# First attention with one cos/sin table: rope queries from doubled weight columns, scores over 128 rows

## The chip, the cores and the metric

The kernel runs on one NeuronCore of a Trainium2 chip. The metric is the device time of one execution in microseconds, lower is better. TensorE is called PE here (its weight loads PEld), VectorE DVE, ScalarE ACT, GpSimd POOL and the queue that issues the transfers SP.

## The reference

Three layers on 512 tokens of width 2048, all in float32: a latent attention with 16 heads, a sliding-window attention, and a mixer of stick-breaking attention and a linear recurrence. The change touches the first. Cut to what matters:

```python
proj = h @ w_in                       # c_q 512, c_kv 512, k_rope 64, gate 2048 columns
q = (rmsnorm(c_q, q_norm) @ w_uq).reshape(B, S, 16, 128 + 64)
q_nope, q_rope = q[..., :128], rope(q[..., 128:], positions, 64)
kv = (rmsnorm(c_kv, kv_norm) @ w_ukv).reshape(B, S, 16, 128 + 128)
k_nope, v = kv[..., :128], kv[..., 128:]
k_rope = rope(k_rope, positions, 64)  # one for all heads
s = (q_nope . k_nope + q_rope . k_rope) * 192 ** -0.5      # causal, softmax, times v
# rope, halves x1, x2 of 32 dims: [x1 * cos - x2 * sin, x2 * cos + x1 * sin]
```

The result is multiplied by silu(gate) and goes through an output projection.

## The kernel before, in words

Every float32 matmul of a projection is done as three: each operand is split into a rounded upper part (hi, ACT) and the rest (lo, DVE), and hi x hi, hi x lo and lo x hi are added up in PSUM. Weights come in tiles of 1 MB into two raw buffers, are split in four pieces of 128x512 each (`hi` L465 on ACT, `lo` L475 on DVE), and `multiply` (L482) runs a piece: four chunks of 128 rows, three matmuls of 512 tokens each (L490 to L492). Which columns of the raw buffer a piece reads is said by `raw_piece` (L451).

Each engine runs its own program; the order is written out by hand. `STEPS` (L82) lists the steps of each engine in each phase, and one counting semaphore per engine (T, A, V, G) tells the others how far it is. The phases: `load`, `in` (nine tiles of the input projection, the ninth holding the 64 rope key columns in its upper half), `mla` (16 heads and one more body), and then the output projection and the other two layers. The `mla` body i does the attention of head i-1 and the projections of head i, interleaved:

- PE (`mla_T`, L910): scores of head i-1 for the query blocks 3, 2, 1, 0, each with three matmuls for the 128 nope rows and three for the 64 rope rows (partitions 64 to 127); gate piece 0; transposes of v; gate piece 1; transposes of the probabilities of block 3 (`turn`, L942); gate piece 2; blocks 2 and 1; gate piece 3; QR, the rope queries (the piece holds 64 nope columns too, so that it has 128); block 0; QN; two matmuls with the rotation matrix into `pt[1]` (L968, L969); KN; probabilities times v (PV); V.
- DVE (`mla_V`, L1041): mask, row maximum and its negative for each block, two weight pieces, normalisation of the probabilities, lower halves, the gate, then `qr` copied out of PSUM, its lower half (`qt_lo`), the lower half of the nope queries, `rope_V` (L880: product with the sine, product with the cosine, sum), the lower half of the rotated queries, and keys.
- ACT (`mla_A`, L986): exponentials, the upper halves, tanh for the gate.

In the phase `in` the same rotation is done once for the keys (`in_T` L773, `in_A` L810, `in_V` L834), between the gate pieces of head 0; behind it DVE does two reciprocals (`rq`, `rkv`), two fills and the first pieces of head 0. Cosine and sine come from two angle computations of nine DVE steps each (`angle_V`, L730) and two ACT sines.

Of the kernel before, what the change touches and what calls it, by code (L numbers as in the profile page):

```python
# [14 lines left out]
P = 128  # L15
# [46 lines left out]
NCONST = columns(CONST, [("ident", P), ("ones", P), ("freq", 2), ("eps", 1), ("one", 1), ("rot1", P), ("causal", P),  # L62
# [29 lines left out]
        "T": "norm norms turn rq_tok".split(),  # L92
        "A": ("root hi0 sq0 hi1 sq1 hi2 sq2 cos hi3 sq3 hi4 sq4 sin hi5 sq5 hi6 sq6 hi7 sq7 rot kt_hi root_q "
              "root_kv kr_hi").split(),
        "V": ("rstd ev0 lo0 ev1 lo1 a00 a01 a02 a03 a04 a05 a06 a07 r0 ev2 lo2 ev3 lo3 a10 a11 a12 a13 a14 a15 "
              "a16 a17 r1 ev4 lo4 ev5 lo5 ev6 lo6 ev7 lo7 ev8 kt_lo k_sin k_cos kr kr_lo rq rkv scale z1 z2").split(),
# [8 lines left out]
    "kv": {
        "T": "norm rows dup0 dup1 dup2 dup3 rstd_tok v0 v1".split(),
        "A": "root dup k_hi0 cos sin k_hi1 kd_hi0 kd_hi1 kd_hi2 kd_hi3 v_hi0 v_hi1".split(),
        "V": ("rstd ev0 k_lo0 pos sinks a00 a01 a02 a03 a04 a05 a06 a07 r0 a10 a11 a12 a13 a14 a15 a16 a17 r1 "
              "ev1 k_lo1 ev2 k_sin0 k_cos0 kr0 kd_lo0 k_sin1 k_cos1 kr1 kd_lo1 k_sin2 k_cos2 kr2 kd_lo2 k_sin3 "
              "k_cos3 kr3 kd_lo3 ev3 scale v_lo0 v_lo1 z1 z2").split(),  # L110
        "G": "z1 z2".split(),
    },
    "swa": {
        "T": "s00 s01 s10 s11 t00 t01 pv0 t10 t11 turn pv1".split(),
        "A": ("exp00 exp01 exp02 exp03 sink0 tanh exp10 exp11 exp12 exp13 sink1 pt_hi00 pt_hi01 qt_hi pt_hi10 "
              "pt_hi11 q_hi").split(),
        "V": ("gate mask00 top00 scaled00 minus00 mask01 top01 scaled01 minus01 mask10 top10 scaled10 minus10 "
              "sum0 inv0 norm0 mask11 top11 scaled11 minus11 silu pt_lo00 pt_lo01 sum1 inv1 norm1 q_ev qt_lo "
              "pt_lo10 pt_lo11 q_sin q_cos qr q_lo y").split(),
        "G": "keys sink pair".split(),  # L120
    },
# [9 lines left out]
    "stick": {
        "T": "z t3 t2 t1 t0 lru pv q_norm k_norm vt".split(),
        "A": ("tanh_s abs0 abs1 abs2 abs3 exp ln weights xc_hi w_hi pt_hi3 pt_hi2 pt_hi1 pt_hi0 tanh_l tanh_r "
              "tanh_i q_sq a tanh_a m q_root q_hi k_sq k_root k_hi v_hi").split(),
# [3 lines left out]
              "kn k_lo v_lo").split(),  # L138
# [111 lines left out]
def constants():  # L250
# [14 lines left out]
    c[:, CONST["rot1"]] = rotation(ROPE1, ROPE1)  # L265
# [20 lines left out]
def build(nc, x, positions, sinks, params, consts, w, out):  # L286
# [6 lines left out]
    with ExitStack() as ctx:  # L293
# [29 lines left out]
        with ExitStack() as scope:  # L323
            c_hi, c_lo = sb("c_hi", [P, 2 * RC, S], F32R, scope), sb("c_lo", [P, 2 * RC, S], F32R, scope)
            cos, sin = sb("cos", [P, S], F32, scope), sb("sin", [P, S], F32, scope)
# [15 lines left out]
            angle, turns, acc_q, acc_kv = kn, prob[:, 0:S], acc, prob[:, S:2 * S]  # L341
# [109 lines left out]
        def raw_piece(tile, p):  # L451
            r = raw[:, tile.slot, :]
            if tile.phase == "mla" and tile.k == 1:
                nq, nk = NOPE + ROPE1, NOPE + V1
                uq = r[:, 0:RC * nq].rearrange("p (c n) -> p c n", c=RC)
                ukv = r[:, RC * nq:RC * (nq + nk)].rearrange("p (c n) -> p c n", c=RC)
                return [uq[:, :, nq - P:nq], uq[:, :, 0:P], ukv[:, :, 0:P], ukv[:, :, P:2 * P]][p]
            if tile.phase == "out3":
                p = (p + PIECES // 2) % PIECES
            return r[:, p * PIECE:(p + 1) * PIECE].rearrange("p (c n) -> p c n", n=P)  # L460

        def split(buf, slot):
            return buf[:, slot, :].rearrange("p (c n) -> p c n", n=P)
# [261 lines left out]
        def angles_V(q, psum, freq, cos_arg, sin_arg, tmp):  # L725

            for n, arg in enumerate((cos_arg, sin_arg)):
                angle_V(q, n, psum, freq, arg, tmp)

        def angle_V(q, n, psum, freq, arg, tmp):  # L730
            shift = (0.25, 0.0)[n]
# [7 lines left out]
            q.eng.tensor_scalar(tmp, arg, shift, magic, ALU.add, ALU.add).then_inc(*q.did(f"a{n}1"))  # L739
# [11 lines left out]
            q.eng.tensor_scalar(arg, arg, float(np.pi / 2) * 4 * shift, 3.14159250, ALU.add, ALU.min).then_inc(*q.did(f"a{n}7"))  # L751
# [21 lines left out]
        def in_T(q):  # L773
# [22 lines left out]
            q.eng.matmul(pt[1][:, :], rot_hi[:, :], qr_hi[:, :], start=True, stop=False)  # L796
            q.eng.matmul(pt[1][:, :], rot_hi[:, :], qr_lo[:, :], start=False, stop=True).then_inc(*q.did("turn"))
# [12 lines left out]
        def in_A(q):  # L810
            q.body("in", 0)
            for k in range(KROPE + 1):
# [11 lines left out]
                if k in (2, 4):  # L824
                    q.eng.wait_ge(*q.at(f"V.r{k // 2 - 1}"))
                    q.eng.activation(((cos, sin)[k // 2 - 1])[:, :], (angle[:, :], turns)[k // 2 - 1], ACT.Sin).then_inc(*q.did(("cos", "sin")[k // 2 - 1]))
            q.eng.activation(rot_hi[:, :], c("rot1"), ACT.Copy).then_inc(*q.did("rot"))
# [3 lines left out]
            q.eng.wait_ge(*q.at("V.kr"))  # L831
            copy_hi(q, kr_hi[:, :], turned, "kr_hi")

        def in_V(q):  # L834
            q.body("in", 0)
            for k in range(KROPE + 1):
# [14 lines left out]
                dst = c_raw[:, k % 2, :] if k < KROPE else qr[:, :]  # L851
                q.eng.tensor_tensor(dst, pp[k % 2][:, :], rstd[:, :], ALU.mult).then_inc(*q.did(f"ev{k}"))
# [11 lines left out]
            q.eng.wait_ge(*q.at(f"G.sum{KROPE - 1}"))  # L864
# [14 lines left out]

        def rope_V(q, plain, turned_psum, source, name):  # L880

            q.eng.wait_ge(*q.at(source))
            q.eng.tensor_tensor(turned, turned_psum[:, :], sin[:, :], ALU.mult).then_inc(*q.did(f"{name}_sin"))
            q.eng.tensor_tensor(plain[:, :], plain[:, :], cos[:, :], ALU.mult).then_inc(*q.did(f"{name}_cos"))
            q.eng.wait_ge(*q.at(f"V.{name}_cos"))
            q.eng.tensor_tensor(turned, turned, plain[:, :], ALU.add).then_inc(*q.did(f"{name}r"))
# [23 lines left out]
        def mla_T(q, i, proj, attn):  # L910
# [10 lines left out]
            if attn:  # L921
                q.eng.wait_ge(*q.at("V.kn_lo", i - 1))
                q.eng.wait_ge(*q.at("V.qr_lo", i - 1))
                for b in reversed(range(NB)):
# [3 lines left out]
                    r = slice(P // 2, P)  # L928
# [1315 lines left out]
```

## Time and profile before

| | us |
|---|---|
| median of 3 runs | 2397.55 |
| lowest and highest | 2395.2, 2397.93 |
| profiled execution | 2396.43 |
| its span | 2394.6 |
| PE busy | 2314.2 (97%) |
| DVE busy | 1494.8 (62%) |
| ACT busy | 957.8 (40%) |

Times in the rows are microseconds from the start of the span. PE's matmuls are pipelined: the duration of one is longer than the distance to the next, so the cost of a matmul in a stream is read from the distances between starts. A form like 64*128 names the rows and columns of the weights.

### The profile page before, as it was taken

What the parts mean: (1) busy time and instruction counts of PE and PEld (TensorE: products, weight loads), DVE (VectorE), ACT (ScalarE), POOL (GpSimd) and SP (SyncE); (2) the same over time, 40 slices, a digit from 0 to 9 for tenths busy, and PEclk for the clock granted to TensorE, in tenths of its full rate; (3) what the DMA queues carried; (4) which work ended last, traced back from release to release, by engine and by line L of the source; (5) the groups of instructions that cost most, each with busy time, mean ns of one, the idle gap of its engine ahead of it and who ended that gap; (6) DMA issues with size and microseconds to landing.
All of it is one profiled execution on the core that took longest, in us unless ns stands there. A gap on an engine that the chain in (4) does not pass through costs nothing.

```text
span 2394.6 us, 32256 instructions
## 1 busy us (share of the span) xinstructions
PE 2314.2 (97%) x10724; PEld 1880.1 (79%) x10724; DVE 1494.8 (62%) x2580; ACT 957.8 (40%) x1870; POOL 193.2 (8%) x226
## 2 busy tenths in 40 slices
PE   7999999999999999999999989989999999997999
PEld 5877788777778878888888878867888888885887
DVE  6556666666643377777777753377666766766332
ACT  5333334333422244444444442255344444444222
POOL 4100000000021101000000031140000000002000
PEclk8999999999999999999999989999999999998999
DMA  6322222222353343222222263432323324233633
GB/s 218 104 66 75 71 60 70 74 74 74 110 176 88 123 118 93 79 79 79 79 79 79 63 218 92 140 93 77 111 72 103 99 84 114 71 98 110 186 95 105
DMA packets 379438, 239.21 MB, mean 100 GB/s; under 512 B 4868, under 2 KB 353284, under 8 KB 379398
## 3 DMA queue, kind: packets, MB, share of 16 engines
q1 hardware_dynamic: 379398, 238.71, 34.6%
q8 instruction: 21, 0.34, 0.1%
q14 instruction: 19, 0.16, 0.0%
HBM read 210.12 MB, written 28.57 MB: 100 GB/s over the span
## 4 chain that ended last, share of the span: by engine, by line
PE 91%; DVE 6%; ACT 1%; POOL 1%; issue 1%; DMA 0%; SPq 0%; DVEq 0%; ACTq 0%
PE pp L490 26%; PE pp L492 25%; PE pp L491 25%; PE ps L511 3%; PE ps L512 2%; PE ps L513 2%; POOL act_lo L1157 1%; DVE act_lo L1756 1%; PE pt L948 1%; DVE w_lo L479 1%; PE po L511 1%; PE po L513 1%; PE po L512 1%; DVE act_lo L709 1%; PE po L1486 1%
## 5 line engine op out<-in xcount | busy, mean ns | idle before, releaser
L490 PE MATMUL pp<-act_hi,w_hi 128*128 128x512 f32 x2496 | 1006.2, 403 | 30.8 <-POOL act_lo L1157 10.2
L492 PE MATMUL pp<-act_hi,w_lo 128*128 128x512 f32 x2496 | 980.2, 393 | 0.0
L491 PE MATMUL pp<-act_lo,w_hi 128*128 128x512 f32 x2496 | 977.7, 392 | 0.0
L479 DVE TENSOR_TENSOR w_lo<-raw,w_hi 128x512 fp32r<-128x512 f32 x692 | 475.0, 725 | 250.2 <-ACT w_hi L473 249.3
L490 PEld LDWEIGHTS pp<-act_hi,w_hi 128*128 128x128 f32 x2496 | 471.8, 189 | 146.0 <-issue 25.1
L492 PEld LDWEIGHTS pp<-act_hi,w_lo 128*128 128x128 f32 x2496 | 471.3, 189 | 102.8
L491 PEld LDWEIGHTS pp<-act_lo,w_hi 128*128 128x128 f32 x2496 | 472.9, 189 | 96.9 <-issue 5.0
L473 ACT ACTIVATE w_hi<-raw 128x512 fp32r<-128x512 f32 x692 | 397.1, 620 | 87.0 <-DMA raw<-w_out 53.7
L1157 POOL TENSOR_TENSOR act_lo<-y_whole,act_hi 128x512 fp32r<-128x512 f32 x36 | 49.1, 1397 | 1132.3 <-ACT act_hi L1151 1132.3
L1541 ACT ACTIVATE s_prob<-ps,s_minus,s_q_scale 128x256 f32<-128x256 f32 x128 | 70.9, 558 | 140.8 <-DVE s_minus L1614 140.8
L1261 DVE TENSOR_TENSOR xT<-pp,xT 128x512 f32 (+1 forms) x32 | 22.1, 691 | 167.6 <-PE pp L492 167.6
L1220 ACT ACTIVATE square<-xT 128x512 f32 (+1 forms) x32 | 20.2, 633 | 255.3 <-DVE xT L1261 255.3
L490 PE MATMUL pp<-c_hi,w_hi 128*128 128x512 f32 x256 | 103.3, 404 | 1.2 <-DVE w_lo L479 0.7
L492 PE MATMUL pp<-c_hi,w_lo 128*128 128x512 f32 x256 | 101.7, 397 | 0.0
L491 PE MATMUL pp<-c_lo,w_hi 128*128 128x512 f32 x256 | 101.7, 397 | 0.0
L1001 ACT ACTIVATE prob<-ps,minus,q_scale 128x512 f32<-128x512 f32 (+1 forms) x64 | 39.0, 615 | 126.4 <-DVE minus L1063 126.4
L1284 POOL TENSOR_TENSOR acc<-acc,square 128x512 f32<-128x512 f32 x30 | 38.8, 1293 | 288.6 <-ACT square L1220 288.6
L490 PEld LDWEIGHTS pp<-c_hi,w_hi 128*128 128x128 f32 x256 | 48.6, 190 | 13.6 <-DVE pT_lo L878 1.1
L492 PEld LDWEIGHTS pp<-c_hi,w_lo 128*128 128x128 f32 x256 | 48.4, 189 | 11.8
L491 PEld LDWEIGHTS pp<-c_lo,w_hi 128*128 128x128 f32 x256 | 48.5, 190 | 10.1
L504 ACT ACTIVATE pT_hi<-pt 128x512 fp32r<-128x512 f32 (+1 forms) x64 | 26.2, 436 | 58.3 <-PE pt L948 58.3
L1605 DVE TENSOR_TENSOR ps<-ps,s_con 128x512 f32<-128x512 f32 x64 | 44.4, 694 | 3.4 <-PE ps L513 3.4
(362 smaller groups left out, 2709.3 us busy)
## 6 DMA issues: line engine op xcount, KB each, us to landing
raw<-w_in SPq DMA_DIRECT2D x48, 1024.0 KB, 5.8
raw<-swa_w_in SPq DMA_DIRECT2D x36, 1024.0 KB, 5.6
raw<-mla_w_in SPq DMA_DIRECT2D x25, 1024.0 KB, 5.8
raw<-mla_w_out SPq DMA_DIRECT2D x16, 1024.0 KB, 6.0
raw<-swa_w_out SPq DMA_DIRECT2D x16, 1024.0 KB, 5.9
raw<-w_out SPq DMA_DIRECT2D x16, 1024.0 KB, 7.4
x_feature_major<-xT SPq DMA_DIRECT2D x12, 1024.0 KB, 7.8
xT<-x_feature_major SPq DMA_DIRECT2D x3, 3584.0 KB, 16.4
```

The lines of the kernel that those rows point to most:

```text
L473: q.eng.activation(split(w_hi, tile.piece_slot(p)), raw_piece(tile, p), ACT.Copy).then_inc(s_hi, 1)
L479: q.eng.tensor_tensor(split(w_lo, s), raw_piece(tile, p), split(w_hi, s).bitcast(F32), ALU.subtract).then_inc(s_lo, 1)
L490: q.eng.matmul(psum[:, :], wh, ah, start=start and n == 0, stop=False)
L491: q.eng.matmul(psum[:, :], wh, al, start=False, stop=False)
L492: last = q.eng.matmul(psum[:, :], wl, ah, start=False, stop=stop and n == PIECE // P - 1)
L511: q.eng.matmul(psum, a[0], b[0], start=start, stop=False)
L512: q.eng.matmul(psum, a[0], b[1], start=False, stop=False)
L513: return q.eng.matmul(psum, a[1], b[0], start=False, stop=stop)
L1001: q.eng.activation(prob[:, OFF[b]:OFF[b] + w_], SCORE[b][:, 0:w_], ACT.Exp, bias=minus[:, b:b + 1], scale=q_scale[:, b:b + 1], accum_out=t ...
L1157: q.eng.tensor_tensor(act_lo[:, j, :], y_whole[:, j, :], act_hi[:, j, :].bitcast(F32), ALU.subtract).then_inc(s_ylo_g if j < Y_GPSIMD else ...
L1541: q.eng.activation(s_prob[:, h, b * 2 * P:(b + 1) * 2 * P], BANKS[h][half][:, b % 2 * 2 * P:(b % 2 + 1) * 2 * P], ACT.Exp, bias=s_minus[:, ...
L1605: q.eng.tensor_tensor(bank, bank, band, ALU.add).then_inc(*q.did(f"mask{h}{half}"))
```

## The change: what it does

The rotation matrix and the cosine and sine tables of the first layer go. The rope query piece is made of the 64 rope columns taken twice, so that its product holds x1, x2, x1, x2 in four groups of 32 rows. One table, `rope_table`, holds cos, cos, sin, -sin in these rows: one angle computation with a shift per row (constants `turns` and `phase`) and one sine. The queries are that product times the table, over 128 rows. For the keys the same is done once, with the table times the norm, and the constant `fold` (128x128 of zeros and ones) adds the four groups up so that every group of 32 rows holds the right half of the rotated key; two matmuls with it take the place of the keys' two rotation matmuls. The scores' rope part then runs over all 128 rows. In the heads the two rotation matmuls, three products and sums and one pair of hi and lo go. Weight pieces are read and written through a pattern with one dimension more (`whole`, `twice`). Step tables of other phases are only moved or wrapped anew.

```diff
-            cos, sin = sb("cos", [P, S], F32, scope), sb("sin", [P, S], F32, scope)
+            rope_table = sb("rope_table", [P, S], F32, scope)
-                return [uq[:, :, nq - P:nq], uq[:, :, 0:P], ukv[:, :, 0:P], ukv[:, :, P:2 * P]][p]
+                return [twice(uq[:, :, NOPE:nq]), whole(uq[:, :, 0:P]), whole(ukv[:, :, 0:P]), whole(ukv[:, :, P:2 * P])][p]
...
+        def twice(half):
+            return half.unsqueeze(2).to_broadcast([P, PIECE // P, 2, ROPE1])
+        def whole(chunks):
+            return chunks.rearrange("p c (d n) -> p c d n", d=2)
         def split(buf, slot):
-            return buf[:, slot, :].rearrange("p (c n) -> p c n", n=P)
+            return buf[:, slot, :].rearrange("p (c d n) -> p c d n", n=ROPE1, d=2)
@@ in_T
-            q.eng.matmul(pt[1][:, :], rot_hi[:, :], qr_hi[:, :], start=True, stop=False)
-            q.eng.matmul(pt[1][:, :], rot_hi[:, :], qr_lo[:, :], start=False, stop=True).then_inc(*q.did("turn"))
+            q.eng.matmul(pt[1][:, :], fold_hi[:, :], qr_hi[:, :], start=True, stop=False)
+            q.eng.matmul(pt[1][:, :], fold_hi[:, :], qr_lo[:, :], start=False, stop=True).then_inc(*q.did("fold"))
@@ in_A
-            q.eng.wait_ge(*q.at("V.kr"))
-            copy_hi(q, kr_hi[:, :], turned, "kr_hi")
+            q.eng.wait_ge(*q.at("T.fold"))
+            copy_hi(q, kr_hi[:, :], pt[1][:, :], "kr_hi")
@@ in_V
-                if k in (1, 3):
-                    angle_V(q, k // 2, pt[0][:, :], c("freq", 0), (angle[:, :], turns)[k // 2], root[:, :])
+                    angle_V(q, 0, pt[0][:, :], c("freq", 0), angle[:, :], root[:, :], c("turns", 0), c("phase", 0))
+                if k == 3:
+                    q.eng.wait_ge(*q.at("A.table"))
+                    q.eng.tensor_tensor(scaled_table, rope_table[:, :], rstd[:, :], ALU.mult).then_inc(*q.did("scaled"))
-            rope_V(q, qr, pt[1], "T.turn", "k")
-            sub_lo(q, kr_lo[:, :], turned, kr_hi[:, :], "kr_lo")
+            sub_lo(q, kr_lo[:, :], pt[1][:, :], kr_hi[:, :], "kr_lo")
@@ mla_T
-                    r = slice(P // 2, P)
-                    m = products(q, SCORE[b][:, 0:n], (qr_hi[r, t_], qr_lo[r, t_]), (kr_hi[r, 0:n], kr_lo[r, 0:n]), False, True)
+                    m = products(q, SCORE[b][:, 0:n], (qr_hi[:, t_], qr_lo[:, t_]), (kr_hi[:, 0:n], kr_lo[:, 0:n]), False, True)
-                q.eng.wait_ge(*q.at("V.qt_lo"))
-                q.eng.matmul(pt[1][:, :], rot_hi[:, :], qr_hi[:, :], start=True, stop=False)
-                q.eng.matmul(pt[1][:, :], rot_hi[:, :], qr_lo[:, :], start=False, stop=True).then_inc(*q.did("turn", rest=not attn))
+                q.eng.wait_ge(*q.at("V.qr"))
                 up_piece(KN, pp[1])
+                if not attn:
+                    q.eng.wait_ge(*q.at("T.rq_tok", phase="in", body=0))
+                    q.eng.sem_inc(*q.did("pv"))
@@ mla_A
-                q.eng.wait_ge(*q.at("V.qr_ev"))
-                copy_hi(q, qr_hi[:, :], qr[:, :], "qt_hi")
+                q.eng.wait_ge(*q.at("V.qr"))
+                copy_hi(q, qr_hi[:, :], qr[:, :], "qr_hi")
-                q.eng.wait_ge(*q.at("V.qr"))
-                copy_hi(q, qr_hi[:, :], turned, "qr_hi")
@@ mla_V
-                q.eng.tensor_copy(qr[:, :], pp[1][:, :]).then_inc(*q.did("qr_ev"))
+                q.eng.tensor_tensor(qr[:, :], pp[1][:, :], rope_table[:, :], ALU.mult).then_inc(*q.did("qr"))
-                rope_V(q, qr, pt[1], "T.turn", "q")
-                q.eng.wait_ge(*q.at("A.qr_hi"))
-                sub_lo(q, qr_lo[:, :], turned, qr_hi[:, :], "qr_lo")
```

## Rows read from the trace of the kernel before

**Rows 1.** Chain that ended last, whole span, shares by line.

```profile
by line: PE pp L490 25.8%; PE pp L492 25.3%; PE pp L491 25.2%; PE ps L511 2.9%; PE ps L512 1.7%; PE ps L513 1.7%; POOL act_lo L1157 1.0%; DVE act_lo L1756 0.9%; issue 0.7%; PE pt L948 0.7%; DVE w_lo L479 0.7%; PE po L511 0.6%; PE po L513 0.
```

**Rows 2.** Windows: bounds, length, busy of each engine, PE clock, DMA share, GB/s.

```profile
145.00:168.30 23.30, 18.42 (x72) 13.75 (x71) 17.83 (x24) 7.00 (x12) 0.00 (x0) 0.93 0.30 85
231.47:263.05 31.58, 31.58 (x150) 25.13 (x149) 20.83 (x43) 12.03 (x26) 0.00 (x0) 1.00 0.25 71
```

**Rows 3.** Timeline of PE in one head's scores: start, duration, line, form.

```profile
231.24 0.40 PE L492 MATMUL pp<-c_hi,w_lo 128*128 128x512 f32 x1
231.47 0.39 PE L511 MATMUL ps<-kn_hi,qn_hi 128*128 128x512 f32 x1
...
231.93 0.39 PE L513 MATMUL ps<-kn_hi,qn_lo 128*128 128x512 f32 x1
232.25 0.50 PE L511 MATMUL ps<-kr_hi,qr_hi 64*128 64x512 f32 x1
232.58 0.39 PE L512 MATMUL ps<-kr_lo,qr_hi 64*128 64x512 f32 x1
232.82 0.39 PE L513 MATMUL ps<-kr_hi,qr_lo 64*128 64x512 f32 x1
...
233.42 0.34 PE L512 MATMUL ps<-kn_lo,qn_hi 128*128 128x384 f32 x1
233.59 0.34 PE L513 MATMUL ps<-kn_hi,qn_lo 128*128 128x384 f32 x1
...
236.45 0.28 PE L512 MATMUL ps<-kr_lo,qr_hi 64*128 64x256 f32 x1
236.56 0.27 PE L513 MATMUL ps<-kr_hi,qr_lo 64*128 64x256 f32 x1
...
237.10 0.40 PE L491 MATMUL pp<-act_lo,w_hi 128*128 128x512 f32 x1
```

**Rows 4.** Timelines of DVE and PEld in that head, and the maxima by tile.

```profile
236.87 0.30 DVE L1057 TENSOR_TENSOR ps<-ps,con 128x128 f32<-128x128 f32 x1 [1.30 <-PE ps L513]
...
242.10 0.49 DVE L1075 TENSOR_SCALAR prob<-prob,inv 128x512 f32<-128x512 f32 x1
242.64 0.44 PEld L948 LDWEIGHTS pt<-con,prob 128*128 128x128 f32 x3
L1059 DVE TENSOR_REDUCE top<-ps x60: 290/490/692, 170.4 to 616.5; 128x1 f32<-128x512 f32 x15, 128x1 f32<-128x384 f32 x15, 128x1 f32<-128x256 f32 x15, 128x1 f32<-128x128 f32 x15
```

**Rows 5.** Waits of PE in the run-in, then timelines of DVE and ACT there.

```profile
PE pt L968 <- DVE qr_lo L507: 2.3, 1, 2.3
PE pt L802 <- DVE y_out L869: 1.4, 1, 1.4
140.86 0.69 DVE L883 TENSOR_TENSOR square<-pt,sin 128x512 f32<-128x512 f32 x1 [2.75 <-PE pt L797]
...
158.36 0.68 DVE L1097 COPY qr<-pp 128x512 f32<-128x512 f32 x1
142.91 0.63 ACT L504 ACTIVATE kr_hi<-square 128x512 fp32r<-128x512 f32 x1 [2.94 <-DVE square L886]
```

**Rows 6.** Timeline of PE: projection KN, first and last head's scores; DVE's kn_lo.

```profile
161.19 0.39 PE L490 MATMUL pp<-c_hi,w_hi 128*128 128x512 f32 x1
...
168.32 0.39 PE L511 MATMUL ps<-kn_hi,qn_hi 128*128 128x512 f32 x1
...
641.70 0.39 PE L511 MATMUL ps<-kn_hi,qn_hi 128*128 128x512 f32 x1
261.18 0.69 DVE L507 TENSOR_TENSOR kn_lo<-qr,kn_hi 128x512 fp32r<-128x512 f32 x1 [0.70 <-ACT kn_hi L504]
```

**Rows 7.** Timeline of GpSimd behind the last head.

```profile
654.23 16.74 POOL L1157 TENSOR_TENSOR act_lo<-y_whole,act_hi 128x512 fp32r<-128x512 f32 x12 [525.88 <-ACT act_hi L1151]
```

**Rows 8.** Lower weight parts by tile: in the heads, then in the output projection.

```profile
L479 DVE TENSOR_TENSOR w_lo<-raw,w_hi x120: 677/684/694, 177.5 to 633.0; 128x512 fp32r<-128x512 f32 x120
L479 DVE TENSOR_TENSOR w_lo<-raw,w_hi x63: 676/678/1467, 671.4 to 831.6; 128x512 fp32r<-128x512 f32 x63
```

More of the change, by code:

```diff
@@ L59, in columns @@
     return at
-NCONST = columns(CONST, [("ident", P), ("ones", P), ("freq", 2), ("eps", 1), ("one", 1), ("rot1", P), ("causal", P),
+NCONST = columns(CONST, [("ident", P), ("ones", P), ("freq", 2), ("eps", 1), ("one", 1), ("fold", P), ("turns", 1), ("phase", 1), ("causal", P),
                          ("rot2", P), ("dup", 2 * P), ("rotdup", 2 * P), ("band", 3 * 2 * P), ("strict", P),
@@ L91 @@
     "in": {
[L92 to L96, printed above, removed]
+        "T": "norm norms fold rq_tok".split(),
+        "A": ("root hi0 sq0 hi1 sq1 hi2 sq2 table hi3 sq3 hi4 sq4 hi5 sq5 hi6 sq6 hi7 sq7 kt_hi root_q root_kv "
+              "kr_hi").split(),
+        "V": ("rstd ev0 lo0 ev1 lo1 a00 a01 a02 a03 a04 a05 a06 a07 r0 ev2 lo2 ev3 lo3 scaled ev4 lo4 ev5 lo5 ev6 "
+              "lo6 ev7 lo7 ev8 kt_lo kr_lo rq rkv scale z1 z2").split(),
         "G": "sum0 sum1 sum2 sum3 sum4 sum5 sum6 sum7".split(),
@@ L99 @@
     "mla": {
-        "T": "s3 s2 s1 s0 vt t3 t2 t1 t0 turn pv".split(),
-        "A": "exp3 exp2 exp1 exp0 v_hi pt_hi3 pt_hi2 pt_hi1 tanh pt_hi0 qt_hi qn_hi qr_hi kn_hi".split(),
+        "T": "s3 s2 s1 s0 vt t3 t2 t1 t0 pv".split(),
+        "A": "exp3 exp2 exp1 exp0 v_hi pt_hi3 pt_hi2 pt_hi1 tanh pt_hi0 qr_hi qn_hi kn_hi".split(),
         "V": ("mask3 top3 minus3 mask2 top2 mask1 top1 mask0 top0 minus inv3 norm3 inv0 norm2 norm1 norm0 v_lo "
-              "pt_lo3 pt_lo2 pt_lo1 gate qr_ev pt_lo0 qt_lo qn_lo q_sin q_cos qr qr_lo kn_ev kn_lo y silu v").split(),
-    },
@@ L105 @@
[L105 to L121, printed above, removed]
@@ L131 @@
[L131 to L134, printed above, removed]
[3 rows of a table removed]
-              "kn k_lo v_lo").split(),
+              "pt_lo3 pt_lo2 pt_lo1 gate qr pt_lo0 qr_lo qn_lo kn_ev kn_lo y silu v").split(),
     },
@@ L148 @@
     },
+    "kv": {
+        "T": "norm rows dup0 dup1 dup2 dup3 rstd_tok v0 v1".split(),
+        "A": "root dup k_hi0 cos sin k_hi1 kd_hi0 kd_hi1 kd_hi2 kd_hi3 v_hi0 v_hi1".split(),
+        "V": ("rstd ev0 k_lo0 pos sinks a00 a01 a02 a03 a04 a05 a06 a07 r0 a10 a11 a12 a13 a14 a15 a16 a17 r1 ev1 "
+              "k_lo1 ev2 k_sin0 k_cos0 kr0 kd_lo0 k_sin1 k_cos1 kr1 kd_lo1 k_sin2 k_cos2 kr2 kd_lo2 k_sin3 k_cos3 "
+              "kr3 kd_lo3 ev3 scale v_lo0 v_lo1 z1 z2").split(),
+        "G": "z1 z2".split(),
+    },
+    "swa": {
+        "T": "s00 s01 s10 s11 t00 t01 pv0 t10 t11 turn pv1".split(),
+        "A": ("exp00 exp01 exp02 exp03 sink0 tanh exp10 exp11 exp12 exp13 sink1 pt_hi00 pt_hi01 qt_hi pt_hi10 "
+              "pt_hi11 q_hi").split(),
+        "V": ("gate mask00 top00 scaled00 minus00 mask01 top01 scaled01 minus01 mask10 top10 scaled10 minus10 sum0 "
+              "inv0 norm0 mask11 top11 scaled11 minus11 silu pt_lo00 pt_lo01 sum1 inv1 norm1 q_ev qt_lo pt_lo10 "
+              "pt_lo11 q_sin q_cos qr q_lo y").split(),
+        "G": "keys sink pair".split(),
+    },
     "out2": {
@@ L264, in rotation @@
         return r
-    c[:, CONST["rot1"]] = rotation(ROPE1, ROPE1)
+    half = ROPE1 // 2
+    fold = np.array([[1, 0, 0, 1], [0, 1, 1, 0], [0, 1, 1, 0], [1, 0, 0, 1]], np.float32)
+    c[:, CONST["fold"]] = np.kron(fold, np.eye(half, dtype=np.float32))
+    c[:, CONST["turns"].start] = np.array([0.25, 0.25, 0.0, 0.5])[p // half]
+    c[:, CONST["phase"].start] = 2 * np.pi * np.array([0.25, 0.25, 0.0, 0.5])[p // half]
     rot2 = c[:, CONST["rot2"]] = rotation(HD2, ROPE2)
@@ L339, in build @@
             gate, th = square[:, 0, :], root
-            angle, turns, acc_q, acc_kv = kn, prob[:, 0:S], acc, prob[:, S:2 * S]
+            angle, scaled_table, acc_q, acc_kv = kn, prob[:, 0:S], acc, prob[:, S:2 * S]
             c_raw, rstd_q, root_q = y_out, y_out[:, 0, :], y_out[:, 1, :]
@@ L738, in angle_V @@
             q.eng.wait_ge(*q.at(f"V.a{n}0"))
-            q.eng.tensor_scalar(tmp, arg, shift, magic, ALU.add, ALU.add).then_inc(*q.did(f"a{n}1"))
+            q.eng.tensor_scalar(tmp, arg, turns, magic, ALU.add, ALU.add).then_inc(*q.did(f"a{n}1"))
             q.eng.wait_ge(*q.at(f"V.a{n}1"))
@@ L823, in in_A @@
                     q.eng.activation(square[:, k % 2, :], c_raw[:, k % 2, :], ACT.Square).then_inc(*q.did(f"sq{k}"))
[L824 to L827, printed above, removed]
+                if k == 2:
+                    q.eng.wait_ge(*q.at("V.r0"))
+                    q.eng.activation(rope_table[:, :], angle[:, :], ACT.Sin).then_inc(*q.did("table"))
+            q.eng.activation(fold_hi[:, :], c("fold"), ACT.Copy)
             copy_hi(q, qr_hi[:, :], qr[:, :], "kt_hi")
@@ L878, in in_V @@
             q.eng.memset(pT_lo[:, hidden].bitcast(F32), 0.0).then_inc(*q.did("z2"))
[L880 to L886, printed above, removed]
         def in_G(q):
```

58 lines of the change are left out of this document (33 added, 25 removed), and 3 rows, old and new, of the table STEPS.

## The prediction

> **What bounds the kernel now.** I read the chain of waits first, then the windows by stage, then the timeline of one head. The chain that ended last lies for 76.3% on the three matmul lines of the weight helper, on TensorE (PE) [rows 1]. Within the first attention one head's window of 31.58 us shows PE busy for all of it, VectorE (DVE) for 20.83 and ScalarE (ACT) for 12.03 [rows 2], so what a head costs is what PE issues, not what the others do. The time from the first head's scores, 168.32, to the last head's, 641.70 [rows 6], is 15 periods of 31.56 us.
>
> Busy is not the same as streaming, though. In the timeline of PE the start-to-start distance tells the price of a matmul. Between two 128x512 matmuls over all 128 rows it is 0.23 us (231.24 to 231.47, and twice that to 231.93), at 384 columns 0.17 (233.42 to 233.59) and at 256 columns 0.11 to 0.12 (236.45 to 236.56) [rows 3]. Where the rope part of the scores begins (form 64*128, half the rows) the distance is 0.32, then 0.33 to its second matmul, together 0.19 more than twice 0.23. Going back, the two distances from 232.82 to 233.42 hold 0.60, of which 0.23 and 0.17 are the matmuls' own, 0.20 more [rows 3]. So each change between 128 and 64 rows opens a hole of about 0.195 us, in two halves. There are eight changes in a head, since four query blocks each go there and back, the last back into the gate's projection.
>
> The run-in is bound otherwise. From 145 to the first scores PE is busy 18.42 of 23.30 us, at a mean clock of 0.93 [rows 2]: there it waits on the split and normalisation chains of DVE and ACT, and the longest of its waits is 2.3 us, for the lower half of the rope queries ahead of the rotation [rows 5].
>
> **Part 1: scores over 128 rows.** The number and the columns of the matmuls stay: 24 per head. Without holes the section would take 6 x (0.231 + 0.173 + 0.118 + 0.118) = 3.84 us. Measured from 231.47 to 237.10, the second matmul of the gate behind it, it is 5.63; less the one 0.231 distance of the gate that lies in it, 5.40 [rows 3]. Difference 1.56 us a head: 8 x 0.195. A matmul over twice the rows is taken at the same time, since the 128-row ones of the same block and columns stream at 0.23, 0.17 and 0.12 and the third rope matmul (232.58 to 232.82, 0.24) isn't faster for having half the rows [rows 3]. Bounds of this part: 0 (the holes stay, for a reason other than the rows) and 1.56; I take 1.56, because the step from the projection's buffers to the scores', 231.24 to 231.47, also changes every operand and has no hole.
>
> Here the Trainium skill has a rule. TensorEngine Tiling (Array Packing), Key Properties, says that a change of tiling mode, not merely of tile, drains TensorE; it gives no price, and the holes of [rows 3] are what it would look like. By it the sum is the same.
>
> **Part 2: what is late next.** Softmax starts from the end of the scores: DVE's mask of block 1 runs at 236.87 after an idle 1.30 us that PE ends, and the normalisation of block 3's probabilities runs from 242.10 for 0.49, to 242.59. PE's weight load for the transposes of that block starts at 242.64, right behind it [rows 4]. So PE already reaches these transposes just as they become ready. Everything from the mask to the normalisation moves with the scores' end, and so does PE's way there (gate piece 0, four transposes of v, gate piece 1), except that the last of the eight holes lies on PE's way and not on the mask's: it is gone for PE alone. PE therefore arrives 0.19 us earlier than the probabilities and waits that long. Is the mask still released by the scores, now that they end 1.4 us sooner behind block 3's? The last matmul of the section would start at 231.47 + 3.84 - 0.12 = 235.19, and the mask 0.31 behind it (236.56 to 236.87 now), at 235.50. DVE's work on blocks 3 and 2 stands ahead: two masks of 0.30, two maxima of at most 0.69 [rows 4] and a one-column step, which I estimate at 0.2, 2.2 us. It starts behind block 3's last matmul, which begins at 231.47 + 5 x 0.231 = 232.63, by 0.31 and 0.11 for twice the columns (256/2.4 GHz): 233.05, and ends at 235.25. It just holds, by 0.25 us. I take 0.2 lost a head, bounds 0 and 0.5 (0.3 more if DVE isn't done). Net of parts 1 and 2: 1.36 a head.
>
> **Part 3: the rotation goes.** Two matmuls of 128x512 a head at 0.23 each [rows 3]: 0.46 us of PE. Nothing waits there in a steady head. The new wait in its place, KN's projection on DVE's product of the queries with the table, stands behind QN's twelve matmuls, 2.8 us after QR's end, where the product takes one DVE step as the copy does now (0.68, [rows 5]); it is met with about 2 us to spare. DVE loses four 0.69 us steps a head (two products, a sum, one subtraction) and ACT one copy of 0.63. All are hidden under PE and count nothing, apart from this: kn_lo, for which the next scores wait, now ends at 261.87 [rows 6], 1.2 us ahead of them (231.47 + 31.56 = 263.03), and will have over 2 us.
>
> Steady head: 31.56 - 1.36 - 0.46 = 29.74. Over 15 periods 27.3 us. The range of a period is 29.4 (no new wait, 0.2 better, and a little) to 30.2.
>
> **Part 4: the first head and what stands before it.** Two steps. In the keys' chain DVE's three products after the fold vanish: ACT's kr_hi starts at 142.91 now and could start when the first product does, 140.86 [rows 5]. That is 2.05 us off a chain that runs on DVE through two reciprocals and six weight splits to QR, QN and the gate, the 1.4 us wait of the transposes [rows 5] being a part of the same delay. So QR, QN and the queries' step end 2.05 sooner: 158.36 + 0.68 - 2.05 = 156.99. KN waits for that, not for the subtraction and rotation behind it; it begins at 161.19 now [rows 6], so 4.15 us earlier, with 1.0 us of the old 2.3 us wait left. Then the clock. From KN's first matmul to the first scores 24 matmuls take 168.32 - 161.19 = 7.13 us [rows 6], 5.55 at 0.231, and the granted clock of this stretch is 0.93 [rows 2]: part of the 24, right after the 2.3 us wait, ran at 1.2 instead of 2.4 GHz. With the longest wait at 1.0 us I take full speed, 1.58 saved, for a total of 5.7. Bounds: 2.5 (the chain is held by the weight splits' ACT side, and the clock falls as before) and 6.5 (the 1.0 wait gone too).
>
> The second angle computation (nine DVE steps) and second sine go, and one product for the scaled table comes: they lie under the nine input tiles, where PE doesn't wait. Value 0, bounds 0 and 0.5.
>
> **Part 5: the last head's tail.** Its scores also shorten, by 1.5 us. Behind them PE isn't the bound: the chain goes softmax, transposes, ACT, and from 654.23 through GpSimd's 12 subtractions, 16.74 us [rows 7]. It starts from the scores' end, so it moves with it, unless the stored y arrives too late (it is asked for independently of the scores). I take 1.4; bounds 0 and 1.6.
>
> **Part 6: weight splits everywhere.** All 692 pairs of hi and lo now go through a pattern with one more dimension, and the rope piece reads each half chunk twice. In the heads, where half of the pieces read a strided source, a lo takes 684 ns; in the first output stage, all contiguous, 678 [rows 8]. The pattern costs 6 ns at most, so I take 0; bounds 0 and 0.05 us a piece, which PE hides in the heads. The chain of waits has the lo's line for 0.7% of the span [rows 1], 16.8 us or 24.5 pieces, so that even the upper bound costs 1.2 us there, and 1.6 more in part 2's softmax (2 pieces in each of 16 heads).
>
> **Sum** in the profiled execution: 27.3 + 5.7 + 1.4 = 34.4 us off a span of 2394.6, that is 2360.2, and 1.8 around it as now (2396.43 - 2394.6) gives 2362.0. The median of the three runs is 1.1 above the profiled one: 2363.1.
>
> **Rivals.**
> A. *The holes stay.* They could belong to a switch of operands rather than of rows. Then 15 x 0.46 + 5.7 = 12.6: 2385. Against it: a change of all operands at full rows is seamless (part 1). Chance 0.07.
> B. *The softmax takes it back.* If DVE's work on blocks 3 and 2, or ACT's exponentials, sets the mask and not the scores' end, PE waits at the transposes for most of the 1.56. With 1.0 a head lost instead of 0.2: 15 x 0.8 = 12 less gained, 2375. For it: the margin of 0.25 us in part 2 and a load that starts 0.05 behind the normalisation. Chance 0.12.
> C. *Slower: the splits.* If the extra dimension or the doubled read costs x us a piece, the loss is (24.5 + 32) x. It outweighs 34.4 from x = 0.61, so nearly a doubling of 0.68; at exactly double, 38 us, 2401. The strided row against the contiguous one speaks against it [rows 8]. Chance 0.03.
> D. *Slower: weight loads of full height show.* If the load of a 128-row weight could not lie under the matmul before it, 12 loads of 0.19 in 16 heads would add 36 us: 2399. The kn matmuls load the same height in the same section at 0.23 apart (231.47 to 231.93). Chance 0.01. The Trainium skill, TensorE: Matmul & The Clock Gate, The mechanism (Part 3), does say that weight loads overlap running matmuls only where their row group differs; this trace disagrees, with 0.23 us between matmuls of one row group, each with a load of its own.
> E. *The doubling isn't what it says*, the rotation gone and something of equal size in its place, or a wait that I don't see: within 0.2% of now. Chance 0.02.
> My forecast has the remaining 0.75, its own range 2358 to 2370.
>
> **Range and chances.** A measurement of this kernel tells about 0.2% (4.8 us) from no change. The range for 8 in 10: down to 2356 (no new wait, 3 us; run-in and tail at their best, 1; and 3 for a run's level), up to 2376, which takes B in and leaves A, C, D and E out with what the forecast's own range misses. Faster: forecast, A and B, 0.94, and half a point of the rest; same 0.02; slower 0.04.
>
> **What would show it.** In the profile after: the rope matmuls' form is 128*128 and all of a block's six start at equal distances; the scores' section is 3.8 to 3.9 us from first to next projection; a head takes 29.7; PE waits 0.2 at the transposes of block 3, released by DVE's normalisation. The first scores start near 162.6, with a granted clock near 1.00 before them. Splits still take 0.62 and 0.68. Wrong would be: a hole that stays at the change from qn to qr weights (A); a wait of near 1 us at the transposes (B); a first head at half clock, which takes 1.6 back.

## The result, and the profile after

| | before, us | changed, us |
|---|---|---|
| median (4 runs each) | 2397.74 | 2359.8 |
| lowest and highest | 2395.2, 2398.92 | 2358.55, 2361.89 |
| profiled execution | 2396.43 | 2360.93 |
| its span | 2394.6 | 2359.1 |

The ratio of changed to before is 0.9844, 95% interval 0.9827 to 0.9861: 1.6% faster, 35.5 us in the two profiled executions. The forecast was 2363, with 2356 to 2376.

The windows of the run-in and of one head, as in [rows 2] (bounds, length, busy of PE, PEld, DVE, ACT, POOL, PE clock, DMA share, GB/s):

```profile
145.00:162.63 17.63, 16.23 (x71) 12.29 (x69) 13.11 (x20) 4.71 (x7) 0.00 (x0) 1.00 0.30 88
221.87:251.49 29.62, 29.62 (x148) 24.72 (x146) 18.27 (x38) 11.41 (x25) 0.00 (x0) 1.00 0.26 75
```

A head now takes 29.62 us, all of it PE's; DVE has gone from 20.83 to 18.27 and ACT from 12.03 to 11.41, which bought nothing by itself (the runs below show it). The run-in to the first scores is 17.63 instead of 23.30 us long, at the full granted clock. The timeline of PE in the scores of that head, to be laid beside [rows 3], with the start of the transposes of v behind the gate piece:

```profile
221.64 0.40 PE L503 MATMUL pp<-c_hi,w_lo 128*128 128x512 f32 x1
221.87 0.39 PE L522 MATMUL ps<-kn_hi,qn_hi 128*128 128x512 f32 x1
...
222.33 0.39 PE L524 MATMUL ps<-kn_hi,qn_lo 128*128 128x512 f32 x1
222.55 0.39 PE L522 MATMUL ps<-kr_hi,qr_hi 128*128 128x512 f32 x1
222.78 0.39 PE L523 MATMUL ps<-kr_lo,qr_hi 128*128 128x512 f32 x1
223.01 0.39 PE L524 MATMUL ps<-kr_hi,qr_lo 128*128 128x512 f32 x1
...
223.40 0.34 PE L523 MATMUL ps<-kn_lo,qn_hi 128*128 128x384 f32 x1
223.58 0.34 PE L524 MATMUL ps<-kn_hi,qn_lo 128*128 128x384 f32 x1
...
225.60 0.28 PE L524 MATMUL ps<-kr_hi,qr_lo 128*128 128x256 f32 x1
...
225.95 0.40 PE L502 MATMUL pp<-act_lo,w_hi 128*128 128x512 f32 x1
...
228.46 0.60 PE L939 MATMUL pt<-con,acc 128*128 128x128 f32 x4
```

The rope products (kr, qr) have the form 128*128. From the last nope product to the first rope one it is 0.22 us (222.33 to 222.55), where it was 0.32, and back (223.01 to 223.40, two distances) 0.39 instead of 0.60. From 221.87 to 225.95 the section takes 4.08, which is 3.85 without the gate's first matmul, against 5.40.

DVE, PE and PEld in that head, as in [rows 4]:

```profile
225.92 0.30 DVE L1057 TENSOR_TENSOR ps<-ps,con 128x128 f32<-128x128 f32 x1 [0.44 <-PE ps L524]
...
231.15 0.49 DVE L1075 TENSOR_SCALAR prob<-prob,inv 128x512 f32<-128x512 f32 x1
...
231.41 0.39 PE L503 MATMUL pp<-act_hi,w_lo 128*128 128x512 f32 x1
231.69 0.42 PEld L949 LDWEIGHTS pt<-con,prob 128*128 128x128 f32 x4 [0.31 <-DVE prob L1075]
232.11 0.48 PE L501 MATMUL pp<-act_hi,w_hi 128*128 128x512 f32 x1
```

The mask still follows PE (idle 0.44 us, released by the scores). The normalisation of block 3 ends at 231.64 and the weight load for its transposes, which in an unbroken stream would start with the matmul of 231.41, starts at 231.69 after an idle 0.31 us. That is the new wait.

The run-in, as in [rows 5] and [rows 6]: PE's waits, ACT's kr_hi, KN's first matmul, the first and the last head's scores, and GpSimd behind the last head, as in [rows 7]:

```profile
PE pp L501 <- DVE qr L1097: 0.8, 1, 0.8
140.77 0.60 ACT L515 ACTIVATE kr_hi<-pt 128x512 fp32r<-128x512 f32 x1 [0.82 <-PE pt L807]
156.92 0.50 PE L501 MATMUL pp<-c_hi,w_hi 128*128 128x512 f32 x1 [0.79 <-DVE qr L1097]
...
162.63 0.39 PE L522 MATMUL ps<-kn_hi,qn_hi 128*128 128x512 f32 x1
...
606.89 0.39 PE L522 MATMUL ps<-kn_hi,qn_hi 128*128 128x512 f32 x1
618.09 16.74 POOL L1155 TENSOR_TENSOR act_lo<-y_whole,act_hi 128x512 fp32r<-128x512 f32 x12 [489.75 <-ACT act_hi L1149]
```

The span's 35.5 us by these marks: the first scores come 168.32 - 162.63 = 5.69 us sooner; 15 periods take 606.89 - 162.63 = 444.26 instead of 473.38, 29.12 less (29.617 a head against 31.559); from the last head's scores to GpSimd's first subtraction it is 11.20 instead of 12.53, 1.33 less. That makes 36.1. Everything behind, which the change doesn't touch, took 0.6 longer in this execution.

### The profile page after: what moved, and what is told of

Same layout as the page of the kernel before. It is cut to its first block, busy times and chain, and to the rows that moved or that the text cites. A ratio compares the mean times of both kernels' runs of the same rounds, so it can differ in the third digit from the quotient of the medians.

```text
span 2359.1 us, 32060 instructions
## 1 busy us (share of the span) xinstructions
PE 2277.1 (97%) x10692; PEld 1868.9 (79%) x10692; DVE 1441.4 (61%) x2505; ACT 947.6 (40%) x1853; POOL 193.8 (8%) x226
## 4 chain that ended last, share of the span: by engine, by line
PE 90%; DVE 6%; ACT 1%; POOL 1%; issue 1%; DMA 0%; SPq 0%; DVEq 0%; ACTq 0%
PE pp L501 26%; PE pp L503 26%; PE pp L502 26%; PE ps L522 2%; PE ps L523 2%; PE ps L524 2%; POOL act_lo L1155 1%; DVE act_lo L1754 1%; PE pt L949 1%; DVE w_lo L490 1%; PE po L522 1%; PE po L523 1%; PE po L524 1%; DVE act_lo L720 1%; PE po L1486 1%
## 5 line engine op out<-in xcount | busy, mean ns | idle before, releaser
L518 DVE TENSOR_TENSOR s_pT_lo<-pt,s_pT_hi 128x512 fp32r<-128x512 f32 x64 | 36.9, 618 | 18.2 <-ACT s_pT_hi L515 18.2
```

## The experiments

Each gives the time of one execution unless a median is named. The run-in's start drifts from run to run by up to 1.4 us (the first of the matmuls that sum the latent norms starts at 135.62 us in the changed kernel's first profile, at 137.05 in its second), so times in the first head are told from there.

**Half of the rows again.**

```diff
+ r = slice(64, 128)
- (qr_hi[:, t_], qr_lo[:, t_]), (kr_hi[:, 0:n], kr_lo[:, 0:n])
+ (qr_hi[r, t_], qr_lo[r, t_]), (kr_hi[r, 0:n], kr_lo[r, 0:n])
```

> The changed kernel, but the rope products of the scores take rows 64 to 127 alone (half of the rope sum is left out). Everything else, the missing rotation included, stays. My theory (each change of the number of rows opens a hole of 0.195 us on PE): eight holes a head are back, the section of the scores takes 5.4 us instead of 3.85, a head 31.1 instead of 29.62, and the profiled execution 2361 + 15 x 1.45 + 1.3 = 2384 us. Rival (the holes came with the old rope operands, queries that passed a rotation and a sum): no holes, 29.6 a head, 2361 us.

Measured: 2386.4 us, a head 31.10. The timeline of PE at the first change of rows:

```profile
225.76 0.40 PE L524 MATMUL ps<-kn_hi,qn_lo 128*128 128x512 f32 x1
226.09 0.50 PE L522 MATMUL ps<-kr_hi,qr_hi 64*128 64x512 f32 x1
226.42 0.39 PE L523 MATMUL ps<-kr_lo,qr_hi 64*128 64x512 f32 x1
```

0.33 and 0.33 again: the holes are back, without any rotation in the kernel. The section of the scores takes 5.40 us as before (225.31 to 230.94, less 0.23), and a head 1.49 more than in the changed kernel. The rival falls.

**The lower half.** The same edit with `slice(0, 64)`.

> As the run on the upper half, but with rows 0 to 63 (the other half of the rope sum is left out). My theory (the number of rows counts, not where they lie): the same as with the upper half, 31.1 us a head and 2384. Rival (a product that starts at row 64 is what stalls): rows 0 to 63 begin where the full products begin, so no holes, 29.6 a head and 2361.

Measured: 2386.3 us, a head 31.09.

```profile
225.60 0.39 PE L524 MATMUL ps<-kn_hi,qn_lo 128*128 128x512 f32 x1
225.92 0.49 PE L522 MATMUL ps<-kr_hi,qr_hi 64*128 64x512 f32 x1
226.25 0.39 PE L523 MATMUL ps<-kr_lo,qr_hi 64*128 64x512 f32 x1
```

The same 0.32 and 0.33. What counts is that the number of rows changes, not where the half lies.

**Part 1 alone, in the kernel before.**

```diff
- r = slice(P // 2, P)
+ r = slice(0, P)
```

> The kernel before, with its rotation, but the rope products of the scores run over all 128 rows (rows 0 to 63 add products that don't belong to the scores). This is part 1 of the change alone. My theory: no holes, the section 3.85 us, 0.1 of it given back as a wait at the transposes of block 3, a head 31.56 - 1.44 = 30.1 us, the first head as before (first scores at 168.3), the profiled execution 2396.4 - 15 x 1.44 - 1.3 = 2373.5. Rival (the holes need the rotation gone too): 2396.

Measured: 2374.0 us, a head 30.07, first scores where they were. 1.49 us a head come from the rows alone, and of the time 22.6 us (2396.56 for the run of before beside it, less 2374.0) of the 35.5.

**Four changes of rows instead of eight.** The kernel before, products sorted:

```diff
- for b in (3, 2, 1, 0): nope(b), rope(b)
+ nope(3), nope(2), rope(3), rope(2), rope(1), nope(1), nope(0), rope(0)
```

> The kernel before, rope products on 64 rows as before, but in another order: nope 3, nope 2, rope 3, rope 2, rope 1, nope 1, nope 0, rope 0. That is four changes of rows instead of eight with the same 24 products. My theory: price per change 0.195, so 0.78 off a head, section 4.62 instead of 5.40, a head 30.8, 2396.4 - 15 x 0.78 = 2384.7, and 0.8 less in the last head, 2384; up to 0.3 a head may come back, because block 3 is ready later (2388). Rival (each rope group costs its two halves, wherever it stands): no gain, 2396.

Measured: 2383.8 us, a head 30.77: 0.79 less than before, 0.198 for each change left out. The timeline of PE where two rope groups follow each other, and where the rows change back:

```profile
232.09 0.39 PE L513 MATMUL ps<-kr_hi,qr_lo 64*128 64x512 f32 x1
232.32 0.34 PE L511 MATMUL ps<-kr_hi,qr_hi 64*128 64x384 f32 x1
...
233.09 0.28 PE L513 MATMUL ps<-kr_hi,qr_lo 64*128 64x256 f32 x1
233.30 0.39 PE L511 MATMUL ps<-kn_hi,qn_hi 128*128 128x256 f32 x1
233.52 0.28 PE L512 MATMUL ps<-kn_lo,qn_hi 128*128 128x256 f32 x1
```

Rope 3 to rope 2 is 0.23 us, no hole; rope 1 to nope 1 is 0.21 and 0.22 where 256 columns take 0.12. The price belongs to the change and not to the rope group. This is also the smaller cure: an order of issue alone gives a good third of the change (12.8 of 35.5 us, one execution beside one of before at 2396.56).

**The first head's wait as it was.**

```diff
  up_piece(QN, pp[0])
- q.eng.wait_ge(*q.at("V.qr"))
+ q.eng.wait_ge(*q.at("V.qr_lo"))
  up_piece(KN, pp[1])
```

> The changed kernel, but PE waits ahead of KN for the lower half of the rope queries (as the old rotation did) instead of for the product alone. In a steady head this wait is met (29.62 a head stays). In the first head it ends 1.5 us later (156.9 to 158.4 us), so PE's wait there is 2.3 instead of 0.8. My theory of the first head (4.1 us of the 5.7 from the shorter chain, 1.6 from the clock, which fell after a wait of 2.3): the clock falls again, and the first scores start at 162.6 + 1.5 + 1.6 = 165.7, granted clock about 0.94 there; 2364 us. Rival (the clock has to do with something else in the old run-in, for instance the longer wait of the transposes ahead): full clock, 164.1, 2362.4.

Measured: 2363.4 us, a head 29.62. PE's wait and the window from KN to the first scores, then the first two matmuls in it:

```profile
PE pp L501 <- DVE qr_lo L518: 2.3, 1, 2.3
158.84:166.00 7.16, 7.16 (x25) 5.75 (x25) 3.04 (x5) 0.78 (x2) 0.00 (x0) 0.77 0.57 149
158.84 0.80 PE L501 MATMUL pp<-c_hi,w_hi 128*128 128x512 f32 x1 [2.31 <-DVE qr_lo L518]
...
160.28 0.63 PE L501 MATMUL pp<-c_hi,w_hi 128*128 128x512 f32 x1
```

The granted clock over these 24 matmuls is 0.77 (0.76 in the kernel before, 1.00 in the changed one), and the first seven of them take 0.63 us or more: from 159.43 on they start 0.43 apart instead of 0.23, the half rate, 1.2 GHz. KN starts 1.52 us later than in the changed kernel, counted from the norms, and the first scores 2.97 later: the 1.45 between is the clock. So of the 5.69 us about 4.25 belong to the shorter chain and 1.45 to the clock (forecast 4.15 and 1.58).

**The rotation's two matmuls.** In that same kernel:

```diff
  q.eng.wait_ge(*q.at("V.qr_lo"))
+ q.eng.matmul(pt[1][:, :], fold_hi[:, :], qr_hi[:, :], start=True, stop=False)
+ q.eng.matmul(pt[1][:, :], fold_hi[:, :], qr_lo[:, :], start=False, stop=True)
```

> The changed kernel, with the wait for the lower half of the rope queries and two 128x512 matmuls of them with the fold matrix ahead of KN, whose result nobody reads. Against the run with that wait alone it prices the rotation's two matmuls. My theory: 0.46 us a head, 30.08 instead of 29.62, and 16 x 0.46 = 7.4 us in all: 2371.5. Rival (PE has room, or the matmuls cost more by what they disturb): 29.6, or over 30.3 a head.

Measured: 2372.4 us, a head 30.08 against 29.62: 0.459 us. In the two single executions the difference is 9.0 us. Of it 15 x 0.459 = 6.9 lie in the periods and 0.4 in the first head; the remaining 1.7 come behind the last head's scores, and I can't place them.

**Plain weight pieces.** `twice` and `whole` taken out, `split` and the pieces as before.

> The changed kernel with the weight pieces read and written by the old pattern and nothing read twice: the rope piece holds 64 nope columns in its lower half again (so queries and keys are other numbers). Everything else as changed. My theory: the extra dimension and the double read are free, the splits take 0.62 and 0.68 us as in both kernels, 2361 within 1.5 us. Rival (they cost some ns a piece that the chains between the stages show): 1.5 to 5 us faster, 2356 to 2359.

Measured: 2363.8 us, a head 29.62, no gain. The time lies 1.3 us above the expected band, on the side away from the rival; in this execution the norms started 1.15 us later than in the changed kernel's profile. The lower weight parts by tile (count: min/median/max), of this kernel and then of the changed one:

```profile
L490 DVE TENSOR_TENSOR w_lo<-raw,w_hi x120: 681/684/693, 171.6 to 599.8; 128x512 fp32r<-128x512 f32 x120
```

```profile
L490 DVE TENSOR_TENSOR w_lo<-raw,w_hi x120: 678/685/694, 170.5 to 598.7; 128x512 fp32r<-128x512 f32 x120
```

684 and 685 ns; ACT's upper parts, in the same order, 627 and 628. The extra dimension and the double read cost nothing that these rows could show.

**The normalisation earlier.** DVE's idle stretch ahead of the two weight pieces is used:

```diff
- up_lo(0); up_lo(1); inv3; norm3; inv0; norm2
+ inv3; norm3; up_lo(0); up_lo(1); inv0; norm2
```

> The changed kernel, with DVE's reciprocal and normalisation of block 3 moved ahead of its two weight pieces, into an idle stretch of 2.3 us. My theory of the new wait (the transposes of block 3 come 0.11 us late because this normalisation stands behind the two pieces): the wait goes, a head takes 29.5 instead of 29.62, 1.8 us in all, 2358. Rival (the next link, the lower parts of v and of block 3's probabilities, is as late): no change.

Measured: a head 29.509 instead of 29.622 in the changed kernel's profile beside it; medians 2359.94 (ratio to before 0.9844, 0.9829 to 0.9859) and 2361.34 (0.9850, 0.9835 to 0.9865). The times alone don't tell them apart; the period does, 0.11 us in the mean of 15. PEld's load then follows without a gap:

```profile
231.61 0.19 PEld L503 LDWEIGHTS pp<-act_hi,w_lo 128*128 128x128 f32 x1
231.84 0.58 PEld L949 LDWEIGHTS pt<-con,prob 128*128 128x128 f32 x4
```

**Both orders.** As above, and in the first head:

```diff
- up_lo(0..3); next_lo(0); next_lo(1); gate; next_lo(2); qr
+ up_lo(0); gate; up_lo(1..3); next_lo(0); next_lo(1); next_lo(2); qr
```

> As the one before, and in the first head DVE computes the gate behind its first weight piece instead of behind six. My theory: the waits of QN (0.5 us) and of KN (0.8 us) in the first head go, the first scores start at 161.2 instead of 162.63, 2357. Rival (DVE's later pieces become late instead): 162 or later.

Measured: median 2357.92 (0.9836, 0.9823 to 0.9850). The waits of 0.5 and 0.8 us are gone, and the first scores come 25.20 us behind the norms instead of 27.01: 1.8 less where 1.4 was expected. A wait costs more than the idle time in its row: that is counted from the modelled end of the matmul before, 0.17 us later than the next would have started, and the first distance behind a wait is 0.34 instead of 0.23 (156.92 to 157.26).

**The same cure in the second attention.**

```diff
- pairk_hi, pairk_lo: [P, S], keys in both halves
+ pairk_hi, pairk_lo: [P, 2, S], rows 0 to 63 of [0] and 64 to 127 of [1], the rest zero
- (s_q_hi[r, t_], s_q_lo[r, t_]), (pairk_hi[r, k], pairk_lo[r, k])       r: the head's 64 rows
+ (s_q_hi[:, t_], s_q_lo[:, t_]), (pairk_hi[:, h, k], pairk_lo[:, h, k])
```

> The changed kernel, and the same cure in the second attention, which the change doesn't touch: its scores are products over 64 rows for each of two heads of a pair. Here GpSimd lays the keys out twice, once with the lower and once with the upper half zero (two tiles, so four half-height copies instead of two), and all products run over 128 rows; the result is the same. My theory: there are four changes of rows in a pair (in and out of two bursts of scores; between the two heads the products overlap by 0.11 us and lose as much again), 0.77 us a pair, 16 pairs, 12.3 us: a pair 28.4 instead of 29.2, 2361 - 12 = 2349, ratio to before 0.980. Rival (DVE, busy 23 of 29 us there, or the softmax chain takes it back, or the keys come too late): 2356 to 2362, with a new wait of PE in the second attention.

Measured: median 2359.51 (0.9842, 0.9826 to 0.9859), within 2 us of the changed kernel's two medians; from the first pair's scores to the last's 453.3 instead of 456.3 us, 0.20 a pair and not 0.77. My sum was wrong. The timeline of PE in the changed kernel, in and around the first of a pair's two bursts of scores (18 products):

```profile
915.20 0.39 PE L503 MATMUL pp<-act_hi,w_lo 128*128 128x512 f32 x1
915.52 0.38 PE L522 MATMUL ps<-pairk_hi,s_q_hi 64*128 64x256 f32 x1
...
916.57 0.28 PE L524 MATMUL ps<-pairk_hi,s_q_lo 64*128 64x256 f32 x1
916.58 0.39 PE L522 MATMUL ps<-pairk_hi,s_q_hi 64*128 64x256 f32 x2
916.80 0.29 PE L523 MATMUL ps<-pairk_lo,s_q_hi 64*128 64x256 f32 x2
916.92 0.29 PE L524 MATMUL ps<-pairk_hi,s_q_lo 64*128 64x256 f32 x2
...
917.82 0.40 PE L502 MATMUL pp<-act_lo,w_hi 128*128 128x512 f32 x1
```

and the same place with full rows:

```profile
915.82 0.40 PE L503 MATMUL pp<-act_hi,w_lo 128*128 128x512 f32 x1
916.05 0.28 PE L522 MATMUL ps<-pairk_hi,s_q_hi 128*128 128x256 f32 x1
...
918.44 0.39 PE L502 MATMUL pp<-act_lo,w_hi 128*128 128x512 f32 x1
```

The rows from 916.57 on are the answer. The kernel issues twelve products of one head (rows 0 to 63) and then six of the next (rows 64 to 127). The first head's ninth product (916.57) and the first of the next row (916.58) start 0.01 us apart, and at 916.80 and at 916.92 two products start together (x2, and busy for hardly longer than one; the x2 at 916.58 is two with starts 0.12 apart, busy 0.39). So three pairs run side by side. That one product of each pair is the first head's and the other the second's I infer from the order of issue, since the rows don't name the half. In all, 18 products take 15 places of 0.12 us. From the last matmul ahead to the second one behind it takes 2.62 us in both kernels (915.20 to 917.82, 915.82 to 918.44). The two holes are paid for by three products that cost no time.

Only the second burst, one head alone, gains, 0.37 (1.55 us from 920.15 to 921.70 in the changed kernel, 1.18 from 920.74 to 921.92 with full rows). The second attention's own rotation, now reached sooner, gives about 0.2 of that back: its weight load waits for DVE, and the two distances at 938.13, 938.46 and 938.79 are 0.33 instead of 0.23.

```profile
938.46 0.19 PEld L1517 LDWEIGHTS pt<-s_q_hi,s_rot 128*128 128x128 f32 x1 [0.37 <-DVE s_pT_lo L518]
```

The Trainium skill, TensorEngine Tiling (Array Packing), Key Properties, says that different tiles can run matmuls in parallel; this trace agrees, with the 0.01 us between starts. I had read the overlap of the two heads as one of 0.11 us that is lost again.

**The changed kernel again**, beside the last runs.

> The changed kernel once more, beside the next three on the same chip: 2360, ratio to before 0.984 to 0.985.

Measured: median 2361.34 (0.9850, 0.9835 to 0.9865), a head 29.62. It is the same kernel, 1.5 us above its first median, and the measure for the versions with one order, both orders and everything, which ran beside it.

**All together:** both orders and the second attention's full rows.

> Both orders and the second attention over full rows together. My theory: the gains add up, 2361 - 12 - 1.8 - 1.4 = 2345 for a profiled execution, ratio to before 0.978, faster than both kernels. Rival: what the second attention gains alone (2349).

Measured: median 2355.21 (0.9824, 0.9811 to 0.9838), five runs from 2354.5 to 2356.8, where the changed kernel beside it had 2359.6 to 2363.4 in four. 6.1 us less than the changed kernel, in the traces 1.7 from the normalisation, 1.8 from the first head and 3.0 from the second attention. It beats both kernels, but 2345 was expected: that sum held 12 us for the second attention, which gave 3.

## Why the prediction was right

**Holes at changes of rows (part 1).** Right in cause and size: section 3.85 for 3.84 forecast, and by order of issue, by row range and in the kernel before the same 0.19 to 0.20 us a change. Rival A is excluded by the two runs on half the rows. What the engine does in these 0.2 us no run shows; that it belongs to a change between 64 and 128 rows, and not to a change of half, is borne out by the second attention, where the stream goes from one half to the other without a hole.

**The softmax (part 2).** Right in place and cause, too large in size: forecast 0.2 lost a head, measured 0.11. From the last projection matmul ahead of block 3's transposes to the first one behind them it is 0.70 us after (231.41 to 232.11) and was 0.59 before (242.60 to 243.19), and the run with the normalisation moved forward has 0.58. The timeline of PE in the kernel before, there and at the transposes of v:

```profile
239.65 0.60 PE L938 MATMUL pt<-con,acc 128*128 128x128 f32 x4
...
242.60 0.39 PE L492 MATMUL pp<-act_hi,w_lo 128*128 128x512 f32 x1
242.83 0.60 PE L948 MATMUL pt<-con,prob 128*128 128x128 f32 x4
243.19 0.48 PE L490 MATMUL pp<-act_hi,w_hi 128*128 128x512 f32 x1
```

My sum put the lateness of the weight load onto the matmuls one for one. But the load had a lead: before, it started 0.19 ahead of its transposes (242.64 and 242.83), after, both start at 231.69. The load is late, and the lead takes up about half of it. The size of this term makes 0.09 of the 0.12 by which the period is shorter than forecast (29.62 for 29.74), 1.4 us over 15 heads, the main part of the error. The rest lies in a place that my sum put at nothing: from the gate's second matmul to the transposes of v it is 2.55 us with half rows (237.10 to 239.65 before, 230.94 to 233.49 in the run on the upper half) and 2.51 with full rows (225.95 to 228.46). So the gate's matmuls behind the last change take 0.04 us more in all; why, no run shows.

The margin of 0.25 us that DVE was to keep before block 1's mask was 0.44. Rival B, which lived on that margin, didn't come.

**The rotation (part 3).** 0.46 forecast, 0.459 measured, and the 2 us to spare for the products of the table stood. Fewer steps on DVE and ACT gave nothing beyond that: the kernel before with full rows, all of its steps kept, takes 30.07 a head, and the changed kernel with two matmuls put back but without those steps 30.08.

**The first head (part 4).** 5.7 forecast, 5.69 measured; the split in chain and clock is shown by the run with the old wait. That the sum fits to 0.01 is luck: the chain gave 0.1 more than forecast (KN's first matmul comes 25.55 us behind the norms before and 21.30 after), the clock 0.15 less (the 24 matmuls take 5.71 at full clock, where I had 5.55). Of the three products that left the keys' chain the trace shows kr_hi at 140.8 for 142.91. KN's wait was forecast as 1.0; its row says 0.8, and from start to start it costs 0.95 (155.74 to 156.92, less 0.23).

**The tail (part 5)**: 1.4 forecast, 1.33. **The pieces (part 6)**: nothing forecast, nothing found; rivals C and D are out, the first by the plain-pieces run, the second by 0.23 us between full-height products, each with its own load.

The sum came to 34.4 us, the marks in the trace to 36.1, the spans to 35.5. That the median fell by 37.9 and not by 35.5 lies within the runs' own spread: before's fourth run was 2398.92, and two of the changed kernel's four lie 2.3 below its profiled one.

## What to carry to other kernels

Where matmuls on 64 rows alternate with matmuls on 128 in one stream, each change costs about 0.2 us of TensorE, at 256 columns as at 512; fill the rows, or sort the products so that the changes are few, before counting anything else. But ask first whether neighbouring half-height products lie in different halves: then they run side by side and may already pay for the holes, and filling the rows takes that away. And read a stream by the distances between starts and by rows that hold two matmuls: the busy share showed 100% of a head that had 1.5 us of holes in it.

## What I had not expected of the hardware

A wait of 2.3 us in place of one of 0.8 is enough to lose the clock here. After waits of 0.5 and 0.8 us the granted clock is 1.00, after one of 2.3 us it is 0.76 to 0.77 over the 24 matmuls from KN to the first scores, in each of the four profiles that have that wait and go on with KN right behind it or behind the rotation (before, its two variants, the old wait in the changed kernel). What differs is where the slow matmuls lie. In the changed kernel with the old wait they are the first seven, at once behind the wait; in the kernel before, PE first goes on for 1.0 us at full rate (160.61 to 161.65), and only then come eight matmuls at the half rate. With the two matmuls of the pricing run the slow stretch begins at once too and takes these two and five more, so that the 24 took 6.56 us, against 7.16 and 5.71. And half-height products of two heads run side by side at 256 columns, three pairs in each first burst, in a kernel that was never written for it.
